# Layer norms by bn statistics, long products finished bank by bank, and a start in smaller pieces, in a two-block transformer kernel

## The reference, cut to what matters

```python
def layer_norm(x, g, b):
    xf = x.astype(f32)
    mu = jnp.mean(xf, -1, keepdims=True)
    var = jnp.mean(jnp.square(xf - mu), -1, keepdims=True)
    return ((xf - mu) * lax.rsqrt(var + LN_EPS) * g + b).astype(x.dtype)
...
        x = layer_norm(DEEPNORM_ALPHA * x + g1 * (y_l @ w_out[l]), ln1_g[l], ln1_b[l])
        x = layer_norm(DEEPNORM_ALPHA * x + g2 * swiglu(x * (1.0 + sc2) + sh2, w_ffn_gate[l],
                                                        w_ffn_up[l], w_ffn_down[l]), ln2_g[l], ln2_b[l])
```

## Time and profile before

| what | us |
|---|---|
| median of 3 runs | 1655.48 (1652.51 to 1659.06) |
| the profiled execution | 1655.95 |
| its span | 1654.2 |
| mean granted TensorE clock | 0.973 of full speed |

### The profile page before, as it was taken

One profiled execution on the slowest core, in us unless ns is written; L12 is line 12 of the kernel. 1 busy time (PEld: TensorE's weight loads), 2 busy tenths in 40 slices (PEclk: granted clock), 3 DMA queues, 4 the chain that ended last, 5 costly groups with the idle time before them and its releaser, 6 DMA issues.

```text
span 1654.2 us, 22991 instructions
## 1 busy us (share of the span) xinstructions
PE 1534.9 (93%) x9387; PEld 1051.1 (64%) x9387; DVE 687.3 (42%) x1457; ACT 382.0 (23%) x846; POOL 212.9 (13%) x362
## 2 busy tenths in 40 slices
PE   7999999999899797888998899999999999999996
PEld 3558755554676464556676578865678854888742
DVE  2205312432544334634443457778778742200003
ACT  1001145321421112232242122143333410100000
POOL 2000000000000000133314000001455530200000
PEclk9999999999999898899999999999989999999998
DMA  9444422565599999999999923441243343343530
GB/s 312 161 152 153 153 103 102 206 198 200 222 406 406 406 407 412 365 417 417 416 411 417 400 77 139 153 140 65 76 192 124 133 153 126 129 153 127 178 127 25
DMA packets 124029, 370.43 MB, mean 224 GB/s; under 512 B 10507, under 2 KB 26517, under 8 KB 107413
## 3 DMA queue, kind: packets, MB, share of 16 engines
q1 hardware_dynamic: 118277, 361.13, 57.7%
q0 software_dynamic: 1280, 6.29, 1.0%
q10 hardware_dynamic: 4368, 1.54, 0.4%
HBM read 367.89 MB, written 1.05 MB: 223 GB/s over the span
## 4 chain that ended last, share of the span: by engine, by line
PE 44%; DMA 6%; DVE 5%; issue 1%; ACT 1%; SPq 0%; ACTq 0%; DVEq 0%
PE psum L2126 27%; PE psum L664 8%; DMA ring<-in_w_down 3%; DMA ring<-in_w_up 3%; PE psum L1921 2%; PE psum L2120 1%; PE psum L1943 1%; PE psum L690 1%; PE psum L1962 1%; PE psum L1905 1%; PE psum L844 1%; DVE area L2534 1%; PE psum L2274 1%; DVE ring L1361 0%; PE psum L823 0%
## 5 line engine op out<-in xcount | busy, mean ns | idle before, releaser
L2126 PE MATMUL psum<-ring,area 128*128 128x512 f32 (+1 forms) x1040 | 449.8, 591 | 7.2 <-DVE area L1384 2.1
L2126 PE MATMUL psum<-area,ring 128*128 128x256 f32 (+1 forms) x1856 | 398.9, 375 | 3.5 <-DMA ring<-in_w_in 1.8
L2126 PEld LDWEIGHTS psum<-area,ring 128*128 128x128 f32 x1856 | 341.7, 191 | 50.6 <-DMA ring<-in_w_in 2.6
L2126 PEld LDWEIGHTS psum<-ring,area 128*128 128x128 f32 x1040 | 197.1, 192 | 244.1 <-issue 241.5
L664 PEld LDWEIGHTS psum<-area 128*128 128x128 f32 x1216 | 145.2, 197 | 21.3 <-issue 15.9
L664 PE MATMUL psum<-area 128*128 128x128 f32 x1216 | 153.7, 284 | 4.3 <-ACT area L1066 4.1
L2399 ACT ACTIVATE area<-psum 128x512 f32<-128x512 f32 x108 | 61.5, 599 | 389.5 <-PE psum L2126 330.3
L1921 PE MATMUL psum<-ring,area 128*32 128x256 f32 x1760 | 111.6, 399 | 23.4 <-DMA ring<-in_w_up 23.4
L1921 PEld LDWEIGHTS psum<-ring,area 128*32 128x32 f32 x1760 | 56.8, 113 | 66.0 <-issue 36.6
L1270 DVE SCALAR_TENSOR_TENSOR area<-area,cols 128x268 f32<-128x268 f32 (+1 forms) x186 | 91.6, 492 | 6.6
L2120 PE MATMUL psum<-const,area 128*128 128x128 f32 x506 | 80.5, 286 | 13.7 <-ACT area L1044 4.1
(11 more groups left out here) (337 smaller groups left out, 1476.6 us busy)
## 6 DMA issues: line engine op xcount, KB each, us to landing
ring<-in_w_in SPq DMA_DIRECT2D x29, 2048.0 KB, 8.3
ring<-in_w_gate SPq DMA_DIRECT2D x55, 1024.0 KB, 15.2
ring<-in_w_up SPq DMA_DIRECT2D x55, 1024.0 KB, 15.3
ring<-in_w_down SPq DMA_DIRECT2D x53, 1024.0 KB, 15.5
ring<-in_w_ada SPq DMA_DIRECT2D x12, 2048.0 KB, 8.0
ring<-in_w_out SPq DMA_DIRECT2D x6, 2048.0 KB, 8.5
area<-in_w_down SPq DMA_DIRECT2D x11, 1024.0 KB, 16.2
ring<-in_w_ffn_gate SPq DMA_DIRECT2D x5, 2048.0 KB, 7.8
```

The source lines that it names most:

```text
L2126: last = nc.tensor.matmul(dst, lhs(k), rhs(k), start=first and k == 0, stop=final and k == count - 1)
```

## The change

It has three parts.

1. **Layer norms.** The residual add is a plain add followed by `bn_stats` over 512 elements; `bn_aggr` makes mean and variance of both halves. The subtraction of the mean, the square sums and the sums are gone; mean and reciprocal root go into two `scalar_tensor_tensor` steps. Token tile 1 is begun only after tile 0 is done. GpSimd's scaling of x gets one more step for each tile, and waits for both tiles' `h_ffn`. The last tile of the output is made and stored in two halves.
2. **Long products.** The last two pieces are multiplied bank by bank: each bank gets both before the next bank is begun.
3. **The start.** x comes in two DMAs on SyncE's queue, each with its signal, and `in0` in two halves behind it with a signal each and no wait for x; the small tables move to ScalarE's queue, g_mix first with a signal of its own, and only g_mix is turned before `hT`. The rest is turned after `in0`. ScalarE gives a root for each token tile, and issues its small loads only after `in0` has landed.

```diff
+        parts_of = stats[:, 16:40].rearrange("p (t h n) -> p t h n", t=NT, h=2)
+        mean_of = stats[:, 40:44].rearrange("p (t n) -> p t n", t=NT)
...
+                tiles = [sum(n for _, n in unit_source(name)) for name in names]
+                def piece(n, j, w):
+                    t, half, k0 = j // 2, j % 2, sum(tiles[:n])
+                    return product(banks[j], lambda k: lhs[:, k0 + k, t * P:(t + 1) * P],
+                                   lambda k: w[:, k, half * WIDE:(half + 1) * WIDE], tiles[n],
+                                   first=n == 0, final=n == len(names) - 1)
...
+                for n, name in enumerate(names[:-2]):
...
+                    for j in range(len(banks)):
+                        last = piece(n, j, w)
+                    piece_passed(last, name)
...
+                ends = [unit(names[-2])[0], None]
+                for j in range(len(banks)):
+                    last = piece(len(names) - 2, j, ends[0])
+                    if j == len(banks) - 1:
+                        piece_passed(last, names[-2])
+                    if j == 0:
+                        ends[1], = unit(names[-1])
+                    last = piece(len(names) - 1, j, ends[1])
+                    order.close((key, j // 2, j % 2))
+                    last.then_inc(filled, 1)
...
-                link(v.tensor_tensor_reduce(x[:, t, part], x[:, t, part], tmp, 1.0, 0.0, ALU.add, ALU.add,
-                                            row_sums[:, half, t:t + 1]))
...
+                link(v.tensor_tensor(x[:, t, part], x[:, t, part], tmp, ALU.add))
+                link(v.bn_stats(parts_of[:, t, half, :], x[:, t, part]))
...
+                link(v.bn_aggr(mean_of[:, t, :], parts_of[:, t, :, :]))
+                root_ask(mean_of[:, t, 1:2], 1.0, LN_EPS)
...
+            def normed(t, gain, bias, dst, signal, pieces=1):
...
+                root_take(mean_of[:, t, 1:2])
+                for part in [slice(i * D // pieces, (i + 1) * D // pieces) for i in range(pieces)]:
+                    link(v.scalar_tensor_tensor(dst[:, part], x[:, t, part], mean_of[:, t, 0:1], gain[:, part], ALU.subtract, ALU.mult))
+                    v.scalar_tensor_tensor(dst[:, part], dst[:, part], mean_of[:, t, 1:2], bias[:, part], ALU.mult, ALU.add)\
+                     .then_inc(s[signal], 1)
...
+                for t in range(NT):
+                    for half in range(2):
+                        residual(key, t, half, gate)
+                    moments(t)
+                    if t == 0:
+                        eng.wait_ge(s["norm_rows_ready"], 1)
+                    normed(t, gain, bias, dst[:, t, :], signal, pieces if t else 1)
...
+            summed("fd", 3, norm_rows[:, 2, :], norm_rows[:, 3, :], x, "x_ready", 2)
...
-                eng.wait_ge(s["h_ffn_ready"], t + 1)
-                link(g.tensor_tensor(x[:, t, :], x[:, t, :], stats[:, 6 + t:7 + t].to_broadcast([P, D]), ALU.mult))
+            eng.wait_ge(s["h_ffn_ready"], NT)
+            for t in range(NT):
+                link(g.tensor_tensor(x[:, t, :], x[:, t, :], mean_of[:, t, 0:1].to_broadcast([P, D]), ALU.subtract))
+                link(g.tensor_tensor(x[:, t, :], x[:, t, :], mean_of[:, t, 1:2].to_broadcast([P, D]), ALU.mult))
...
+            for n, (t, part) in enumerate(((0, slice(0, D)), (1, slice(0, WIDE)), (1, slice(WIDE, D)))):
+                sp.wait_ge(s["x_ready"], n + 1)
+                sp.dma_start(out[0, t * P:(t + 1) * P, part], x[:, t, part]).then_inc(s["out_done"], 16)
...
+                    for half in range(2 if i == 0 else 0):
+                        wait_drained(pe, ("hT", t, half))
+                    if (i, t) == (0, 0):
+                        dst = open_tile(("in", i, t))
+                        product(dst, lambda k: hT[:, k, 0:P], lambda k: w[:, k, :], 4, final=False)
+                        pe.wait_ge(s["in0_rest"], 16)
+                        product(dst, lambda k: hT[:, 4 + k, 0:P], lambda k: w[:, 4 + k, :], 4, first=False).then_inc(filled, 1)
...
-            eng.dma_start(x[:, :, :], a["x"][0].rearrange("(t p) d -> p t d", p=P)).then_inc(s["x_in"], 16)
-            root(stats[:, 0:2])
+            eng.dma_start(rows_a[0:KD, 0, :], a["g_mix"].rearrange("x (a p) -> (x a) p", p=P)).then_inc(s["mix_in"], 16)
...
+                    eng.dma_start(rows_a[first:first + count, which, :], src.rearrange(flat, p=P)).then_inc(s["rows_in"], 16)
...
+            for t in range(NT):
+                root(stats[:, t:t + 1])
+            eng.wait_ge(s["in0_rest"], 16)
...
+            square_sums(x[:, 0, :], xn[:, 0, :], stats[:, 0:1])
+            root_ask(stats[:, 0:1], D)
+            eng.wait_ge(s["x_in_1"], 16)
+            square_sums(x[:, 1, :], xn[:, 1, :], stats[:, 1:2])
+            root_take(stats[:, 0:1])
+            root_ask(stats[:, 1:2], D)
+            normed_x(0)
+            root_take(stats[:, 1:2])
+            normed_x(1)
...
-            sp.wait_ge(s["x_in"], 16)
...
+                        sp.dma_start(dst[:, 0:4, :], rows[:, 0:4, :]).then_inc(landed[unit_slot[name]], 16)
+                        sp.dma_start(dst[:, 4:KD, :], rows[:, 4:KD, :]).then_inc(s["in0_rest"], 16)
...
+                sp.dma_start(x[:, t, :], a["x"][0, t * P:(t + 1) * P, :]).then_inc(s[("x_in", "x_in_1")[t]], 16)
```

More of the change, by code:

```diff
@@ L1634, in normed @@
-            def normed(ss, t, gain, bias, dst, signal):
-                root_take(ss[:, t:t + 1])
-                link(v.scalar_tensor_tensor(dst, x[:, t, :], ss[:, t:t + 1], gain, ALU.mult, ALU.mult))
-                v.tensor_tensor(dst, dst, bias, ALU.add).then_inc(s[signal], 1)
-            def summed(key, gate, ss, gain, bias, dst, signal):
-                for half in range(2):
-                    residual(key, 0, half, gate)
-                centred(ss, 0)
-                residual(key, 1, 0, gate)
-                eng.wait_ge(s["norm_rows_ready"], 1)
-                normed(ss, 0, gain, bias, dst[:, 0, :], signal)
-                residual(key, 1, 1, gate)
-                centred(ss, 1)
-                normed(ss, 1, gain, bias, dst[:, 1, :], signal)
+                link(v.tensor_tensor(x[:, t, part], x[:, t, part], tmp, ALU.add))
@@ L1652, in second_block_dve, with summed @@
+            def summed(key, gate, gain, bias, dst, signal, pieces=1):
+                for t in range(NT):
[5 more added lines that the diff above has]
+                    normed(t, gain, bias, dst[:, t, :], signal, pieces if t else 1)
             eng.wait_ge(s["mod_drained"], 12 - MOD_FIRST)
             eng.wait_ge(s["x_scaled"], 1)
-            summed("w2", 0, stats[:, 6:8], ffn_rows[:, 0, :], ffn_rows[:, 1, :], h_ffn, "h_ffn_ready")
+            summed("w2", 0, ffn_rows[:, 0, :], ffn_rows[:, 1, :], h_ffn, "h_ffn_ready")
@@ L2147, in _ @@
                     transposes(("hT", t, half), [xn[:, t, (4 * half + j) * P:(4 * half + j + 1) * P] for j in range(4)])
-            for t in range(NT):
-                for half in range(2):
-                    wait_drained(pe, ("hT", t, half))
             for i in (0, 1, 2, 3):
```

100 lines of the change are left out of this document (44 added, 56 removed).

## The result

The changed kernel takes 1637.18 us (median of 5 runs, 1635.62 to 1638.08) where the kernel before, run beside it, takes 1655.29 (5 runs, 1652.51 to 1659.06). The ratio is 0.9894, with a 95% interval from 0.988 to 0.9907: 1.06% faster, 17.5 us by the ratio (15.4 to 19.9 by its interval) and 18.1 by the medians. The profiled execution took 1635.62 us, its span is 1633.9, its mean granted clock 0.979 (1655.95, 1654.2 and 0.973 before).

A forecast was written before the change was run, and what follows sets the result against it. TensorE bounds the kernel, held back by weight loads only in the expert stretch. Start 2.8, first norm 3.8 and end 6.1 us sum to 12.7 off 1655.95, giving 1643.25, or 1642.8 as median; range 1638.7 to 1647.2.

The forecast's parts named there:

- The three places: Start before the first product, first layer norm after w2, and end after TensorE's last product: 2.8, 3.8 and 6.1 us won.
- Middle: First layer norm after the w2 product: TensorE's two waits vanish, 3.8 us won, bounds 3.3 to 4.0.
- E + 9.4: E is the w2 product's end; TensorE begins tile 1's `h_ffn` transposes 9.4 us later, where before it was 13.2.
- End: From TensorE's last product to the span's end: 8.5 us instead of 14.6, 6.1 won, bounds 5.0 to 6.8.
- the 5.7 that it would have given: The end's gain in us if the last DMA took 2.7 us from issue, by the skill page's fixed 2.0 us.
- the term of the start: Slow records early in the first product cost 2.9 us before; change in that cost taken as 0, from -0.8 to +1.9.
- Two ways of counting: First product's slow part ends at 18.3 us by slow work done, or 20.0 from the first transpose, costing 0.8 more.
- rival B: At the start, the first product's slow stretch shortens and x's half comes sooner: 2 to 2.5 us more, 1640.5; chance 0.16.
- a start term near 4.5: The start's gain instead of 2.8 us, if a gapless start sped up TensorE's clock sooner, by the skill page.
- A: The start's gain is lost in the weight-bound expert stretch, which starts at its own time: 1645.6; chance 0.14.
- C: New norm operations and halves are dear, `bn_stats` 1.3 us, `bn_aggr` 0.68, x no sooner: 1645.2; chance 0.12.
- D: ScalarE's small loads at the start end too late for `mem`, making the kernel slower; chance 0.03.

The follow-up runs named there:

- the six executions with the old start: Traces of the kernel before (twice), with parts 1 and 2, with each of them alone, and with only GpSimd waiting for both tiles; `mem` transposes at 45.35 us on average.
- the repeated pair of kernels: The changed kernel again, unedited, beside the kernel before: 1635.59 us (6 runs), ratio 0.9895.
- the products alone: The kernel before with only the last two pieces of the long products multiplied bank by bank; norms, GpSimd and start as before: 1646.06 us, ratio 0.9952.
- one moved wait: The kernel before, only that GpSimd waits for both tiles' `h_ffn` before it scales x: 1652.83 us, ratio 0.999.

## Why the prediction came out as it did

**What held.** The three places, and at two of them nearly the sizes. Middle 4.3 against 3.8, above its bound of 4.0: the prediction let TensorE begin the second group at E + 9.4, and it begins at E + 8.9, since both groups begin some 0.15 us before the modelled end of the product ahead of them (1391.58 for 1391.73, 1400.66 for 1400.82) and the sum had rounded up by 0.1; VectorE's chain is E + 5.8 against 5.7. End 6.0 against 6.1: in parts `bn_stats` 0.69 (0.65), `bn_aggr` 0.21 (0.2), half steps 0.75 (0.67), and from VectorE's end to the span's 2.44 (2.7). The two errors there, 0.3 up and 0.3 down, cancel. The Trainium skill (DMA: Bandwidth & Descriptors, Anatomy of one DMA) gives 2.0 us plus the bytes' time for one DMA, measured on GpSimd's queue. The prediction named it without that condition; SyncE's last store of 256 KB landed 2.0 us after its issue in all, so for this queue the measurement decides against that sum, and the term was 6.0, not the 5.7 that it would have given.

**What failed** is the term of the start that the prediction put as "I take 0, from -0.8 to +1.9" for the slow records of the first product. Between the two profiled executions the start's 6.28 us are 3.82 for the earlier beginning (forecast 3.15), less 0.48 for the tables (0.35), plus 30.50 - 28.04 + 0.48 = 2.94 for the slow records (forecast 0). Over all traces they are worth about 2, since they differ from run to run: from the product's start to `mem` the six executions with the old start took 30.50, 30.41, 29.25, 29.23, 29.24 and 29.51 us, 29.7 on average, where 27.56 is the full pace. With the product's own start also taken over all traces (4.0 for the 3.15 forecast), the mis-sized terms of the start are the slow records, put at 0 and worth about 2 us, and the earlier beginning, 0.9 too small. Two ways of counting were worked out there, by slow work done and by time since the first transpose; both took the slow pace for something that has to run off, and a row of 1.00 for proof that it was not the clock. The table of the clock shows that it was: the pace doubles at the moment at which a full clock is first recorded. And the runs refute both ways of counting: the transposes begin at the same time (10.04 to 10.15), and the pace is full from anywhere between 12.81 and 21.85, with slow records in all six traces in which TensorE stood still for 1.7 us or more ahead of the product, and almost none in the eight in which it stood still for 1.1 us or less. This was rival B, with 1640.5 and a chance of 0.16: right in its mechanism, and with about 2 us over all traces (2.94 in the first pair) near its size of 2 to 2.5; its other half, x there sooner, didn't come (4.58 against 4.5). In the sentence on the Trainium skill (TensorE: Matmul & The Clock Gate, Part 1), a start term near 4.5 stood for the rule that TensorE's pace follows how busy it has been; the runs agree with its direction, and 5.6 was measured.

The other 0.67 us of the start in the first pair: 0.24 in VectorE's chain (its tile 0 scaled at 8.25, the transposes at 8.31 for 8.55), 0.14 in the transposes (3.54 for 3.68), and 0.29 between the two: the forecast put the product 0.12 us behind the transposes' end (8.55 + 3.68), and it begins 0.17 before their modelled end of 11.85.

**The rivals.** A, the start's gain lost in the weight-bound stretch: steps that both traces have stay the same distance apart through all of it (VectorE 62.49 and 56.21, 318.46 and 312.18, ScalarE 564.44 and 558.15, 766.06 and 759.86, 889.34 and 883.01): 6.2 to 6.3 us, as at 46 us. The stream of weights starts as much earlier. C: `bn_stats` is not dear (0.69 us, not 1.3). D: 5.9 us of cover are left.

**The range** was drawn from the bounds of the terms, 1638.8 to 1646.6, from a median of three runs. The measured places sum to 5.6 + 4.3 + 6.0 = 15.9 us, which by the forecast's own reckoning is 1639.6, inside the range; 15.4 to 19.9 is what the runs give. Where single executions lie 11 us apart with the granted clock, a median of three carries some 2 us, which belonged on top of the bounds at both ends. Whether the 1.6 us between 15.9 and the ratio's 17.5 (2.2 to the medians' 18.1) are scatter alone, or something small all along the kernel, can't be told from these runs; the repeated pair of kernels gave 18.0 again.

## What to carry to other kernels

Where an engine has work to go on with, one cure is enough and the second gives nothing; at the program's end each saved step counts in full, so finish accumulations bank by bank there. Before a wait of TensorE is priced, look at the records behind it: here a wait of 1.7 to 2.3 us came with 2 us of slow records on top. And where a gain of 1% is looked for in a kernel that scatters by 0.7%, read it at its places between fixed points of both traces, and repeat the kernel before.

## What the runs showed of the hardware that I had not expected

A granted clock of 1.00 in the first 20 us is no proof of the full clock. In the kernel before TensorE ran at half pace there (0.853 us a record for 0.429, 0.213 us a transpose for 0.11), at 1.00 in the row. The row says so only because the trace's table of the clock has nothing there: it begins at 21.46 us, with the full clock, where the pace doubles, and in each of the 14 traces it begins so, between 5.30 and 21.85 us. In the trace of the products alone, with the same start, the clock was full at 13.52 and fell back, and there the rows show the lower level, 0.50 or 1.2 GHz, at the same half pace:

```profile
16.00:18.00 2.00, 2.00 (x4) 0.82 (x4) 0.00 (x0) 0.00 (x0) 0.00 (x0) 0.73 1.06 359
18.00:20.00 2.00, 2.00 (x3) 0.67 (x2) 0.00 (x0) 0.00 (x0) 0.00 (x0) 0.50 1.09 383
22.00:24.00 2.00, 2.00 (x6) 0.85 (x5) 0.00 (x0) 0.00 (x0) 0.00 (x0) 1.00 1.06 362
```

So the slow records are the lower level of the clock, with which TensorE began in every trace here; that the stretch ahead of the table's first row was at that level is read from the pace. When it first rose differed from one execution of the same start to the next, from 13.19 to 21.85 us in the six traces, and with it what the slow records cost, from 1.7 to 2.9 us (29.23 and 30.50 against 27.56). What sets the moment these runs don't show.

After one and the same idle time of 3.2 us, which ends at 1220.49 before and at 1214.67 now, the granted clock fell to 0.50 (1.2 GHz) in one execution and stayed at 1.00 in another. VectorE's steps stretched from 0.75 to 2.47 and from 1.22 to 3.25 us beside GpSimd's, and came back with one moved wait. A store of 256 KB landed in 2.0 us where one of 512 KB took 2.6.
